# A hybrid decoder layer on one core: tangent gates, mask rows ahead of key sums, output blocks between pooled products, stores in 2 KB rows

## What is computed

```python
x = x + 0.5 * swiglu(rmsnorm(x, ffn1_norm), w_gate, w_up, w_down)      # 2816 wide
h = rmsnorm(x, mix_norm)
proj = h @ w_in                       # q, k, v, o, i/f gates, pool channels
q, k = silu(causal_dwconv(q, k))
o_gate = jax.nn.sigmoid(proj_o)
hm = mlstm_chunkwise(q, k, v, i_pre, f_pre)      # 4 heads x 128
hm = hm * lax.rsqrt(jnp.mean(hm * hm, axis=-1, keepdims=True) + EPS)
hm = o_gate * (hm * mh_norm)
hp = multiscale_pool(proj_pool, pool_w, pool_scale)      # 4 groups x 128, windows 2, 4, 8, 16
x = x + concat(hm, hp) @ w_out
x = x + 0.5 * swiglu(rmsnorm(x, ffn2_norm), ...)
return rmsnorm(x, final_norm)
```

## Time and profile before

| | |
|---|---|
| median of 3 runs | 906.07 us (905.74 to 907.24) |
| the profiled execution | 905.26 us |
| its span in the trace | 903.5 us |
| TensorE matmul busy | 888.4 us (98%) |
| VectorE busy | 677.6 us (75%) |
| ScalarE busy | 455.5 us (50%) |
| GpSimd busy | 44.9 us (5%) |
| data moved | 93.84 MB, 104 GB/s |

### The profile page before, as it was taken

The page is one execution under the profiler, slowest core; times in us unless marked ns, Lnnn a source line. Parts: engine busy times, 40 slices in busy tenths (PEclk is TensorE's granted clock), DMA queues, the critical chain, the costliest instruction groups (busy, mean ns, idle before and its releaser), DMA issues.

```text
span 903.5 us, 15533 instructions
## 1 busy us (share of the span) xinstructions
PE 888.4 (98%) x5554; PEld 802.3 (89%) x5554; DVE 677.6 (75%) x1169; ACT 455.5 (50%) x754; POOL 44.9 (5%) x63
## 2 busy tenths in 40 slices
PE   9999999999999999999999999999999999999996
PEld 7899999999888887888887788999999999888886
DVE  7999999998643434677796689899999998634334
ACT  7665665665432323444862365566566665423221
POOL 0000000000000000001535100000000000000000
PEclk9999999999999999999999999999999999999998
DMA  6232333332432323222323232333323332432312
GB/s 245 93 117 95 104 104 112 97 101 85 152 117 93 116 95 115 70 91 84 106 71 103 70 132 70 96 105 104 111 97 103 106 106 81 140 116 97 113 47 94
DMA packets 40188, 93.84 MB, mean 104 GB/s; under 512 B 4436, under 2 KB 6628, under 8 KB 40152
## 3 DMA queue, kind: packets, MB, share of 16 engines
q1 hardware_dynamic: 39832, 92.83, 31.0%
q0 software_dynamic: 176, 0.46, 0.2%
q10 hardware_dynamic: 144, 0.08, 0.0%
HBM read 91.24 MB, written 2.11 MB: 103 GB/s over the span
## 4 chain that ended last, share of the span: by engine, by line
PE 80%; DVE 9%; ACT 4%; issue 3%; POOL 2%; DMA 0%; DVEq 0%; ACTq 0%; SPq 0%; POOLq 0%
PE ps L517 14%; PE ps L519 13%; PE ps L518 13%; PE ps L412 12%; PE ps L414 12%; PE ps L413 12%; DVE work L1630 2%; ACT w_hi L836 1%; PE ps L442 1%; DVE w_lo L1281 1%; PE ps L445 1%; PE ps L448 1%; DVE w_lo L1398 1%; POOL arena L1234 1%; DVE work L1651 1%
## 5 line engine op out<-in xcount | busy, mean ns | idle before, releaser
L1281 DVE TENSOR_TENSOR w_lo<-raw,w_hi 128x1024 fp32r<-128x1024 f32 x83 | 102.6, 1237 | 119.5 <-ACT w_hi L836 113.6
L412 PE MATMUL ps<-act_hi,w_hi 128*128 128x512 f32 (+1 forms) x470 | 179.0, 381 | 0.7 <-DVE act_lo L1762 0.7
L414 PE MATMUL ps<-act_hi,w_lo 128*128 128x512 f32 (+1 forms) x470 | 178.4, 380 | 0.0
L413 PE MATMUL ps<-act_lo,w_hi 128*128 128x512 f32 (+1 forms) x470 | 178.4, 379 | 0.0
L517 PE MATMUL ps<-xg_hi,w_hi 128*128 128x256 f32 x608 | 175.0, 288 | 0.3 <-DVE work L1434 0.3
L519 PE MATMUL ps<-xg_hi,w_lo 128*128 128x256 f32 x608 | 172.3, 283 | 0.0
L518 PE MATMUL ps<-xg_lo,w_hi 128*128 128x256 f32 x608 | 172.0, 283 | 0.0
L836 ACT ACTIVATE w_hi<-raw 128x1024 fp32r<-128x1024 f32 x75 | 79.1, 1056 | 151.4 <-PE ps L414 147.0
L517 PE MATMUL ps<-xe_hi,w_hi 128*128 128x256 f32 x456 | 128.2, 281 | 0.0
L519 PE MATMUL ps<-xe_hi,w_lo 128*128 128x256 f32 x456 | 127.4, 279 | 0.0
L518 PE MATMUL ps<-xe_lo,w_hi 128*128 128x256 f32 x456 | 127.4, 279 | 0.0
(11 more groups left out here) (220 smaller groups left out, 1387.6 us busy)
## 6 DMA issues: line engine op xcount, KB each, us to landing
raw<-weights SPq DMA_DIRECT2D x85, 512.0 KB, 3.3
raw<-weights SPq DMA_DIRECT2D x152, 256.0 KB, 2.6
x<-x_t SPq DMA_DIRECT2D x8, 256.0 KB, 5.6
first<-weights SPq DMA_DIRECT2D x8, 256.0 KB, 5.3
out<-x SPq DMA_DIRECT2D x6, 256.0 KB, 2.4
work<-neg_rows SPq DMA_DIRECT2D x4, 256.0 KB, 3.2
root<-root_rows SPq DMA_DIRECT2D x4, 256.0 KB, 3.8
out<-x SPq DMA_DIRECT2D x4, 128.0 KB, 2.1
```

Source lines behind the costliest of these rows:

```text
L412: pe.matmul(acc, hi, m_hi, start=first, stop=False)
L413: pe.matmul(acc, hi, m_lo, start=False, stop=False)
L414: return pe.matmul(acc, lo, m_hi, start=False, stop=last)
L1281: dve.tensor_tensor(w_lo[:, k % SLOTS], raw[:, k % RAWS], f32(w_hi[:, k % SLOTS]), ALU.subtract).then_inc(lo_made, 1)
```

## The change

It makes these edits:

- **Mean columns.** `mean_columns(1)` moves from ahead of the first q/k unit into it, at k = 2.
- **Head values.** The four key-sum products of `values` follow all four strips, with the wait on GpSimd in front of them.
- **GpSimd.** The mask additions of head h+1 are issued ahead of the key sums of head h.
- **Gates.** sigmoid(z) becomes (tanh(z/2) + 1)/2: tanh on ScalarE, the 1 added in `head_product`, the 1/2 folded with the head's gain into `half_mh`, applied in `mixed_hi` and `mixed_lo`. The table set of exp is preloaded ahead of the heads, that of silu behind them.
- **Denominators.** ScalarE squares the key sums (`square_sum`, 128x4); VectorE's copy and square go, so that 1 of 3 tiny operations of `head_columns` stays. `mixed_hi(h-2)` moves behind `probs_hi` and the split.
- **Pool and output projection.** `pool_mix(0)` moves from ahead of `proj(7)` to k = 2 in it; the other three now each follow the head rows of one output block; the rows of the pooled products follow for the three blocks in turn. ScalarE and VectorE split the weights for it earlier.
- **First pass of the seven-product loop.** VectorE's `act_low` moves ahead of `sum_1` and `sum_3`.
- **Stores.** The last products go to `sums` and `raw` instead of in place, laid out so that two blocks are one row of 2 KB; the output's layout in memory follows and the host turns it back.

```diff
-HSTEPS = STEPS + 3
+HSTEPS = STEPS + 1
...
+        y_half = [t[:].rearrange("p k n -> p (k n)").rearrange("p (d n) -> p d n", n=HALF) for t in (sums, raw)]
...
-                    sp.dma_start(out[d * P:(d + n) * P, at].rearrange("(n p) t -> p n t", p=P),
-                                 x[:, d:d + n, at]).then_inc(stored, 16)
+                    sp.dma_start(out[a, :, d:d + n], y_half[a][:, d:d + n]).then_inc(stored, 16)
...
-                        if S == 0:
-                            pe.wait_ge(ks_made, h + 1)
+                    pe.wait_ge(ks_made, h + 1)
+                    for S in range(TB):
                         mm = pe.matmul(ps_col[:, SUMW * S:SUMW * (S + 1)], key_sum[:, S * P:(S + 1) * P],
...
                 def head_mean(h):
                     pe.wait_ge(sqn_made, h + 1)
-                    pe.wait_ge(hcol_step, HSTEPS * h + 1)
+                    pe.wait_ge(qsq_made, h + 1)
...
+                        if i == 7 and k == 2:
+                            pool_mix(0)
...
-                mean_columns(1)
+
+                def mean_hook(k):
+                    if k == 2:
+                        mean_columns(1)
...
                 proj(6)
-                pool_mix(0)
                 proj(7)
-                pool_mix(1)
...
-                part(0, (0, 1, 2, 3), first=True)
-                pool_mix(2)
-                part(0, (7, 6))
...
+                for d in range(3):
+                    pe.wait_ge(lo_made, WO_UNIT + d + 1)
+                    part(d, (0, 1, 2, 3), first=True)
+                    pool_mix(d + 1)
+                for ks in ((7, 6), (5,), (4,)):
+                    for d in range(3):
+                        part(d, ks, last=ks == (4,))
...
+                act.preload_act_table_set("exp_and_others")
...
-                    act.activation(gate_of[h % 2], gate_of[h % 2], ACT.Sigmoid).then_inc(o_made, 1)
+                    act.activation(gate_of[h % 2], gate_of[h % 2], ACT.Tanh, scale=0.5).then_inc(o_made, 1)
...
+                def square_sum(h):
+                    act.wait_ge(num_made, h + 1)
+                    if h >= 1:
+                        act.wait_ge(hcol_step, HSTEPS * (h - 1) + 2)
+                    act.activation(dcol[:], ps_col[:, 0:SUMW * TB:SUMW], ACT.Square, scale=ROOT_EPS
+                                   ).then_inc(qsq_made, 1)
...
+            masked_rows(0)
+            for h in range(HEADS):
+                if h + 1 < HEADS:
+                    masked_rows(h + 1)
+                key_sums(h)
...
-                    then(dve.tensor_copy(qcol[:], ps_col[:, 0:SUMW * TB:SUMW]))
-                    then(dve.scalar_tensor_tensor(dcol[:], qcol[:], EPS, qcol[:], ALU.mult, ALU.mult))
...
-                    dve.scalar_tensor_tensor(t1[h % 2], ps_num, scalar_of(V_MH + h), gate_of[h % 2],
-                                             ALU.mult, ALU.mult).then_inc(t1_made, 1)
+                    dve.scalar_tensor_tensor(t1[h % 2], gate_of[h % 2], 1.0, ps_num,
+                                             ALU.add, ALU.mult).then_inc(t1_made, 1)
...
-                            dve.tensor_tensor(x[:, k, at], x[:, k, at], ps[:, 6, at], ALU.mult).then_inc(yb_made, 1)
+                            dve.tensor_tensor(y_half[a][:, k], x[:, k, at], ps[:, 6, at], ALU.mult).then_inc(yb_made, 1)
```

More of the change, by code:

```diff
@@ L38 @@
 EPS = 1e-6
+ROOT_EPS = 1e-3
 K_SCALE = float(P) ** -0.5
@@ L143, in build_layer @@
         em2 = sb("em2", [P, TB * HEADS])
+        half_mh = sb("half_mh", [P, HEADS])
         with ExitStack() as ffn_only:
@@ L787, in mixer @@
                 pe.wait_ge(mix_made, HEADS)
-                pe.wait_ge(lo_made, WO_UNIT + 1)
-                part(0, (0, 1, 2, 3), first=True)
-                pool_mix(2)
-                part(0, (7, 6))
[L792 to L798, removed]
-                part(0, (4,), last=True)
-                part(1, (4,), last=True)
-                part(2, (7, 6, 5, 4), last=True)
+                for d in range(3):
[5 more added lines that the diff above has]
+                        part(d, ks, last=ks == (4,))
                 for d in range(3, KD):
@@ L1136, in mixed_hi @@
                     act.wait_ge(hm_made, h + 1)
-                    act.activation(act_hi[:, QK + h], t1[h % 2], ACT.Copy).then_inc(mix_hi_made, 1)
+                    act.wait_ge(half_made, 1)
+                    act.activation(act_hi[:, QK + h], t1[h % 2], ACT.Copy, scale=half_mh[:, h:h + 1]
+                                   ).then_inc(mix_hi_made, 1)
                 def pool_hi(i):
@@ L1164, in mixer @@
                 square_num(0)
+                square_sum(0)
                 gate(0)
@@ L1173, in mixer @@
                     square_num(h)
-                    if h >= 2:
-                        mixed_hi(h - 2)
+                    square_sum(h)
                     if h + 1 < HEADS:
@@ L1178, in mixer @@
                     split_next()
+                    if h >= 2:
+                        mixed_hi(h - 2)
+                act.preload_act_table_set("silu_and_others")
                 mixed_hi(HEADS - 2)
@@ L1184, in mixer @@
                 split_next()
+                split_next()
                 pool_hi(1)
@@ L1225, in _, with masked_rows @@
             pool.dma_start(arena[:, 4], pool_w).then_inc(pw_in, 16)
-            for h in range(HEADS):
+            def masked_rows(h):
                 pool.wait_ge(r_in[h % 2], 16 * (h // 2 + 1))
@@ L1269, in _ @@
                 pool.wait_ge(gained, d + 1)
-                pool.tensor_tensor(x[:, d, 0:HALF], x[:, d, 0:HALF], rinv[:, 0:HALF], ALU.mult).then_inc(ya_made, 1)
+                pool.tensor_tensor(y_half[0][:, d], x[:, d, 0:HALF], rinv[:, 0:HALF], ALU.mult).then_inc(ya_made, 1)
         @block.vector
@@ L1451, in iteration @@
                         sum_3(s + 1)
-                        if head:
-                            act_low(PLAIN[p] - 1)
                         sum_2(s + 1)
@@ L1535, in ffn_up @@
                 plain_product(PLAIN[p] - 1)
+                act_low(PLAIN[p] - 1)
                 iteration(0, 0, head=True)
@@ L1584, in split_next @@
                     nxt[0] += 1
+                dve.tensor_scalar(half_mh[:], vec[:, V_MH:V_MH + HEADS], 0.5, None, ALU.mult).then_inc(half_made, 1)
                 inverse_rms(1)
@@ L1731, in mixed_lo @@
                     dve.wait_ge(mix_hi_made, h + 1)
-                    dve.tensor_tensor(act_lo[:, QK + h], t1[h % 2], f32(act_hi[:, QK + h]),
-                                      ALU.subtract).then_inc(mix_made, 1)
+                    dve.wait_ge(half_made, 1)
+                    dve.scalar_tensor_tensor(act_lo[:, QK + h], t1[h % 2], half_mh[:, h:h + 1],
+                                             f32(act_hi[:, QK + h]), ALU.mult, ALU.subtract).then_inc(mix_made, 1)
                 def pool_in(i):
@@ L1967 @@
     args = [nc.dram_tensor(k, v.shape, F32, kind="ExternalInput").ap() for k, v in arrays.items()]
-    out = nc.dram_tensor("out", (D, T), F32, kind="ExternalOutput").ap()
+    out = nc.dram_tensor("out", (2, P, KD, HALF), F32, kind="ExternalOutput").ap()
     neg_rows = nc.dram_tensor("neg_rows", (HEADS, T), F32, kind="Internal").ap()
@@ L1972 @@
     r = run_bass_kernel_spmd(nc, [arrays], core_ids=[0])
-    return np.ascontiguousarray(r.results[0]["out"].T).reshape(1, T, D)
+    return np.ascontiguousarray(r.results[0]["out"].transpose(0, 3, 2, 1)).reshape(1, T, D)
```

40 lines of the change are left out of this document (17 added, 23 removed).

## The result

The changed kernel takes 900.67 us, the median of 6 runs (900.32 to 901.84), against 906.53 us for the kernel before beside it (6 runs, 904.61 to 908.29): a ratio of 0.9938, 95% interval 0.9924 to 0.9952. It is faster by 0.5 to 0.8%, inside the range of the forecast and 1.5 us above its value. The profiled execution took 900.76 us, its span is 899.0 us. The total hides that two terms of the sum were too large by 0.8 and 1.7 us.

A forecast was written before the change was run, and what follows sets the result against it. TensorE's stream, 98% busy, was taken to set the time; gains of 1.16 + 2.4 + 2.6 + 0.3 = 6.5 us, less 0.4 for thin covers, from 905.26 gave 899.2 us, range 898.0 to 902.2.

The forecast's parts named there:

- Mean columns: Ahead of the first q/k unit: six matmuls run first, so TensorE's wait for the last square goes, 1.16 us.
- Heads: Mixer heads: earlier mask additions and fewer table loads end TensorE's waits for ScalarE's squares, 2.4 us.
- Rivals A and D: Heads: A, mask additions stay slow, waits remain, 901.6 us, 12%; D, key sums late in every head, 908.8 us, 5%.
- Pool and output projection: Pooled products and output projection: the new TensorE order removes three waits for low parts, 2.6 us.
- walking the queues: Pool groups: with everything 3.6 us earlier, low parts are ready 0.7 to 1.6 us ahead of TensorE for four products.
- rival B: Pool groups: GpSimd's window sums are slowest, waits return at pool_mix(0) and pool_mix(2), up to 2.6 us; 901.8 us, 14%.
- Values, 0: Value products of a head: moving the key-sum products costs nothing, bounded at -0.4 to +0.2 us.
- Store, 0.3 us: Last stores: 2 KB rows leave faster than 1 KB rows, 0.3 us, between 0 and 0.5.
- Free edits: act_low ahead of sum_1 worth 0; half_mh is one small operation during a VectorE wait; scaled copies keep their sizes.
- The sum: Whole kernel: 1.16 + 2.4 + 2.6 + 0.3 = 6.5 us gained, with 0.4 given back for thin covers.

The follow-up runs named there:

- e2: Changed kernel with the mean columns ahead of the first q/k unit again; median 901.69 us.
- e3: Changed kernel with GpSimd's mask additions of head h+1 behind the key sums of head h again; median 902.90 us.
- e8: Changed kernel with mixed_hi earlier, VectorE's pool low parts reordered, group 2 scaled earlier and the first pooled product at k = 3; median 897.14 us.
- e6: Changed kernel with mixed_hi(h-2) ahead of probs_hi and the split again on ScalarE; median 898.07 us.
- e9: Changed kernel with act_low behind sum_1 and sum_3 again in the first pass of both seven-product loops; median 900.52 us.
- e7: Changed kernel with VectorE's low part of the first pooled product ahead of group 2's mean, and group 2's low part ahead of the weight split; median 899.99 us.
- e10: Changed kernel with VectorE's copy and square of the key sums back in place of ScalarE's square; median 899.43 us.
- e4: Changed kernel with the sigmoid, its table loads and the old split of the mixed head back; median 903.77 us.
- e5: Changed kernel with pooled products and output projection in the old order on TensorE, ScalarE and VectorE; median 901.79 us.

## Why the prediction was right, and where its steps failed

**Mean columns, 1.16 us: right.** The wait went, and e2 brings it back at 1.16.

**Heads, 2.4 us: 1.6 came.** Beyond the mean columns, TensorE gains 1.35 us at the first head mean, 0.98 at the second and 0.30 at the third, 2.6 in all, and gives 1.0 back at the values of head 3. Both causes named were real: the masks (e3) and the table loads (e4). The additions took 1.73 us for my 2.2, `square_sum` 0.17 for 0.2. Rivals A and D stayed away: ScalarE did wait for the key sums, but TensorE did not. What failed is a part that the sum left out: the move of `mixed_hi(h-2)` behind `probs_hi` and the split, which the change lists, got no price and no look at who waits for it.

**Pool and output projection, 2.6 us: 0.9 came.** The step that failed is "walking the queues with everything 3.6 us earlier, I find the low parts ready 0.7, 1.6, 1.0 and 1.4 us ahead". It assumed that VectorE comes 3.6 us earlier with TensorE; VectorE stood for `mixed_hi`, and its product of the last head (L1732, L1727 before) came only 2.0 us earlier, counted from the gate columns (135.5 us behind them in place of 137.5). The second cause is the order of VectorE's queue together with GpSimd's window sums of group 2, which began 2.8 us later than in e8, counted from that product. For the third pooled product the walk found 1.0 us to spare; group 2's low part was ready 0.9 us late, and the split that frees the PSUM bank 1.6 us late. This is rival B in part, at the two places it named, with 1.9 us of gaps against 2.6 before.

The two failures are mostly one. With `mixed_hi` back (e6) the stretch gains 215.6 - 209.7 = 5.9 us over the kernel before; the forecast had 1.16 + 2.4 + 2.6 - 0.4 = 5.8. The sum was right for a kernel with this one line elsewhere, its parts less so: there the heads gave 2.9 for 2.4 and pool and output projection 1.8 for 2.6, with a gap of 1.13 left, so two errors cancel in it.

**Values, 0: right.** The products of head 0 take 2.71 us in either order.

**Store, 0.3 us: right**, 5.59 against 5.29 on average. The Trainium skill has two rules that bear on it. "DMA: Bandwidth & Descriptors" (Specifications) puts the smallest transfer for line rate at 512 B, by which the term is 0; the measurement does not bear that out. "Perfetto Trace Analysis" (DMA Optimizations) says that small DMAs, under 2 KB, carry a significant overhead; taken as a rule on rows, which the page does not say, it fits the measurement.

**Free edits: right** for `act_low` (e9) as far as can be told; the bunched additions of the output blocks made no wait on TensorE.

**The sum** was 6.1 us. The traces show 3.7 + 0.3 = 4.0 us that belong to the change; 0.5 us less in each network and 0.5 more in the tail norm came with this pair of traces and are not shown to be its doing. The medians of the runs say 5.9 us, the interval of the ratio 4.4 to 6.9. Over the executions beside the experiments it is 5.1: 905.31 us on average in 54 of the kernel before, 900.25 in 18 of the four kernels whose mixer stretch takes 211.9 and whose rows are 2 KB (the changed one, e7, e9, e10). Of those, the ones with a mean granted clock of 0.997 differ by 4.3 us (904.28 in 22, 900.03 in 9), near the 4.0 of the traces. The rest comes with the clock, which is lower in many executions of the kernel before (last section) and for which the prediction has no term.

The forecast subtracts from the traced execution, 905.26 us, which lies at the top of the 903.3 to 905.3 us that the kernel before takes at this clock. Less the 4.0 us of the traces it gives 901.3: still in the range, which takes in rivals A and B, but outside the forecast's own 898.1 to 900.8. That the time landed at 900.67, inside that too, is luck.

## What to carry to other kernels

Price every moved instruction, the small ones too: ask who waits for it and what is queued behind that waiting instruction, and whether a buffer comes free only behind it. Here one high part moved by 2.3 us of ScalarE's queue cost 2.2 us of an expected 5.8, part of it 35 us later. When a stage upstream gets faster, work out again which queues really move with it. Read a small change by stretches of the trace between fixed instructions; these repeated within 0.1 us where whole runs differed by 2. Then compare the executions too: they can differ by something that the one traced execution does not have.

## What the runs showed of the hardware

The granted clock fell behind short waits in some executions and not in others. The tail norm has the same two waits of 1.1 and 1.4 us in all fourteen traces; in eight it took 4.41 us and in six, all with the new store, 4.85 to 4.93. The windows of the changed kernel and of e9_actlow_old over the four spread products (columns as above):

```profile
892.30:893.70 1.40, 1.22 (x4) 0.50 0.00 0
```

```profile
892.60:893.50 0.90, 0.71 (x4) 1.00 0.00 0
```

The same four instructions take 1.22 us at 1.2 GHz and 0.71 at 2.4. In the mixer two of the fourteen traces show such a fall, which cost 1.6 us behind the wait for the mean columns (e2) and 3.4 us in the heads (e4), both in kernels with waits that the changed one lacks. So a wait can cost more than its own length.

How often, the executions tell, each of which has its mean granted clock on record. In the kernel before it is 0.995 or less in 29 of 54 (906.1 us on average) and 0.997 in 22 (904.3). With the wait at the mean columns back (e2) it is 0.995 or less in 2 of 6, with the masks late (e3) in 3 of 9, with the sigmoid (e4) in 5 of 10. In the changed kernel and all others of the experiments, which have no wait at the mean columns or the head means, it is so in none of 41, not even with the old pool order (e5), whose waits reach 1.5 us. So the lower clocks come with the waits that the change removes at the mean columns and in the heads. That they are falls like those in the traces of e2 and e4 is likely but not shown: both traces of the kernel before are of executions at 0.997. Why these waits and not those of the pool groups stays open.
